# Two-block transformer kernel on one core: x also loaded already turned, and a new order for three attention units

## The reference

```python
xn = rms_norm(x, ln_mix_g)                 # x * rsqrt(mean(x*x) + eps) * g
proj = xn @ w_in                           # 1024 x 2560: u, v, q, k, v of attention
a_out = gmlp_spatial_gating(proj[..., :512], proj[..., 512:1024], ...)
b_out = banded_chunk_attention(q, k, v, q_g, k_g, rel_bias)   # 8 heads of 64
x = x + concatenate([a_out, b_out]) @ w_out
x = x + peer_ffn(rms_norm(x, ln_ffn_g), ...)   # each token: 8 heads x 16 rows of a table
# of 16384 x (1024 + 1024) floats, picked by top-k, gathered, dotted, summed
# then a second block: pooling, stick-breaking attention, memory attention, three gates, feed-forward
```

## Time and profile before

| | |
|---|---|
| median of 3 runs | 1152.63 us (1152.09 to 1153.28) |
| the profiled execution | 1152.65 us, of which the span of the engines' work is 1150.8 us |
| PE busy | 1052.1 us (91%), 4100 products |
| DVE busy | 770.2 us (67%) |
| ACT busy | 567.1 us (49%) |
| POOL busy | 288.6 us (25%) |
| gathered by POOL's queue | 268.45 MB, 56.3% of the engines' span |
| loaded by SP's queue | 102.65 MB, 24.1% |

### The profile page before, as it was taken

The page is one execution under the profiler, slowest core; times in us unless marked ns, Lnnn a source line. Parts: engine busy times, 40 slices in busy tenths (PEclk is TensorE's granted clock), DMA queues, the critical chain, the costliest instruction groups (busy, mean ns, idle before and its releaser), DMA issues.

```text
span 1150.8 us, 11796 instructions
## 1 busy us (share of the span) xinstructions
PE 1052.1 (91%) x4100; PEld 669.8 (58%) x4100; DVE 770.2 (67%) x1501; ACT 567.1 (49%) x1235; POOL 288.6 (25%) x261
## 2 busy tenths in 40 slices
PE   8999999998898779799887877889999999999998
PEld 7888554454354234344332322359878778888886
DVE  5788767667666657676676665564675596777743
ACT  7664644444543443643444345354765455444432
POOL 0001445444534424454443444400000000000000
PEclk9999999999999999999999999999999999999999
DMA  9848999999999999999999999977443454555540
GB/s 353 332 164 346 389 421 421 422 421 422 421 421 422 421 421 421 422 420 422 421 422 421 422 421 420 420 305 268 181 147 140 153 192 157 185 185 196 195 154 36
DMA packets 55531, 371.85 MB, mean 323 GB/s; under 512 B 6192, under 2 KB 7344, under 8 KB 12080
## 3 DMA queue, kind: packets, MB, share of 16 engines
q0 software_dynamic: 36864, 268.45, 56.3%
q1 hardware_dynamic: 18608, 102.65, 24.1%
HBM read 370.03 MB, written 1.05 MB: 322 GB/s over the span
## 4 chain that ended last, share of the span: by engine, by line
PE 55%; DMA 30%; DVE 6%; ACT 5%; issue 2%; POOL 1%; DVEq 0%; POOLq 0%; ACTq 0%
DMA uv<-in_peer_uv,eidx 30%; PE bank L2298 13%; PE bank L1980 8%; PE bank L1982 8%; PE bank L1981 8%; PE bank L2474 6%; PE bank L2052 4%; PE bank L2473 3%; DVE uv L1589 3%; DVE w_lo L1300 1%; PE bank L1951 1%; ACT diag L1038 1%; POOL uv L742 1%; ACT chosen L1035 1%; PE bank L2175 1%
## 5 line engine op out<-in xcount | busy, mean ns | idle before, releaser
L2298 PE MATMUL bank<-uv,diag 128*128 128x512 f32 x1024 | 490.1, 613 | 85.2 <-ACT diag L1038 84.8
L1589 DVE SCALAR_TENSOR_TENSOR uv<-uv,xn 128x1024 f32<-128x1024 f32 x256 | 313.7, 1226 | 210.4 <-DMA uv<-in_peer_uv,eidx 210.3
L742 POOL DMA_INDIRECT uv<-in_peer_uv,eidx x256 | 288.3, 1126 | 457.4 <-PE bank L2298 333.2
L2298 PEld LDWEIGHTS bank<-uv,diag 128*128 128x128 f32 x1024 | 183.6, 192 | 354.5 <-ACT diag L1038 200.5
L1300 DVE TENSOR_TENSOR w_lo<-wraw,w_hi 128x2048 fp32r<-128x2048 f32 x69 | 157.6, 2289 | 92.8 <-ACT w_hi L818 92.8
L1030 ACT ACTIVATE chosen<-chosen 128x1 f32<-128x1 f32 x256 | 51.8, 202 | 330.5 <-DVE uv L1589 330.1
L818 ACT CAST w_hi<-wraw 128x2048 fp32r<-128x2048 f32 x69 | 131.6, 1908 | 123.7 <-PE bank L2474 62.0
L2474 PE MATMUL bank<-nT_both,w_hi 128*128 128x512 f32 x320 | 109.6, 396 | 0.0
L1038 ACT ACTIVATE diag<-const,chosen 128x128 f32<-128x128 f32 x256 | 102.8, 401 | 8.3
L1035 ACT ACTIVATE chosen<-chosen 128x1 f32<-128x1 f32 x256 | 75.3, 294 | 9.3
L2473 PE MATMUL bank<-nT_both,w_lo 128*128 128x256 f32 x280 | 78.1, 279 | 0.0
(11 more groups left out here) (332 smaller groups left out, 1372.2 us busy)
## 6 DMA issues: line engine op xcount, KB each, us to landing
wraw<-in_ff_in SPq DMA_DIRECT2D x22, 1024.0 KB, 4.7
wraw<-in_ff_out SPq DMA_DIRECT2D x11, 1024.0 KB, 4.8
wraw<-in_query SPq DMA_DIRECT2D x4, 1024.0 KB, 5.3
uv<-in_peer_uv,eidx POOLq DMA_INDIRECT x256, 15.0
wraw<-in_in_q SPq DMA_DIRECT2D x2, 1024.0 KB, 7.4
wraw<-in_in_k SPq DMA_DIRECT2D x2, 1024.0 KB, 8.8
wraw<-in_pool_o SPq DMA_DIRECT2D x2, 1024.0 KB, 4.8
wraw<-in_sb_o SPq DMA_DIRECT2D x2, 1024.0 KB, 4.8
```

The source lines that it names most:

```text
L742: pool.indirect_dma_start(out=uv[:, ROW_SLOT[n], :], out_offset=None, in_=io["peer_uv"], in_offset=bass.IndirectOffsetOnAxis(ap=eidx[:, he ...
L1589: nc.vector.scalar_tensor_tensor(out=u, in0=u, scalar=1.0, in1=xn[:, head // PEER_HEADS, :], op0=ALU.mult, op1=ALU.mult, accum_out=hdot[he ...
L2298: mm = nc.tensor.matmul(acc[m][:, :], diag[:, n % RING, :], uv[:, ROW_SLOT[n], D + m * HALF:D + (m + 1) * HALF], start=False, stop=(n == R ...
```

## The change

x is brought a second time, turned on the host (`io["xT"]`), in four pieces of 256 KB, into the tile that held the gained values before (`xg`). TensorE's 16 transposes, the four banks that they took and DVE's `gained_T` go. ACT rounds x chunk by chunk (128x128) with the channel's gain as its scale, DVE takes the rest chunk by chunk, also with the gain, and the first triples wait for one chunk each. Chunks and quarters of weights alternate on both engines. `keep_warm` does 11 products where it did 6. in2a and in2b are loaded and split in quarters too. x as it is, needed for the squares, comes after in2b; ACT splits in3a before it reads the first products. The loads of the constants and of some small tensors move back. In the attention, units 0 and 1 are divided before the maxima of unit 2 are taken.

```diff
@@ -63,7 +63,7 @@
-PIECED = ("in1a", "in1b", "in2_vb")
+PIECED = ("in1a", "in1b", "in2a", "in2b", "in2_vb")
@@ -145,7 +145,8 @@
-    uses, count, turn, held = {}, [0] * 8, {}, set()
+    uses, count, held = {}, [0] * 8, set()
+    turn = {tuple(range(8)): NT * 2}
@@ -163,7 +164,6 @@
-    both("xT")
@@ -279,8 +279,7 @@
-    keys = [("xT", t, h) for h in range(2) for t in range(NT)]
-    keys += [("oT", 0), ("aT", 0), ("aT", 1), ("oT", 1)]
+    keys = [("oT", 0), ("aT", 0), ("aT", 1), ("oT", 1)]
@@ -491,6 +490,8 @@
         half_normed = sem("half_normed")
+        xT_loaded = [[sem(f"xT_loaded{t}{h}") for h in range(2)] for t in range(NT)]
+        x_rounded = [sem(f"x_rounded{t}") for t in range(NT)]
@@ -655,22 +656,29 @@
+            def load_xT(t, h):
+                sp.dma_start(xg[:, t, 4 * h:4 * h + 4, :], io["xT"][:, t, 4 * h:4 * h + 4, :]).then_inc(xT_loaded[t][h], 16)
             sp.dma_start(const[:, 0:C0], io["const"][:, 0:C0]).then_inc(ident_loaded, 16)
-            load_x(0)
-            for q in range(2):
+            load_xT(0, 0)
+            for q in range(KC // 2):
                 load_piece("in1a", q)
-            load_x(1)
-            for q in range(2, KC // 2):
-                load_piece("in1a", q)
-            for q in range(KC // 2):
+            load_xT(1, 0)
+            load_piece("in1b", 0)
+            load_xT(0, 1)
+            for q in range(1, KC // 2):
                 load_piece("in1b", q)
-            load_blocks("in2a", "in2b")
-            sp.dma_start(const[:, C0:C0 + 3 * P + 768], io["const"][:, C0:C0 + 3 * P + 768]).then_inc(const_loaded, 16)
+            load_xT(1, 1)
+            for name in ("in2a", "in2b"):
+                for q in range(KC // 2):
+                    load_piece(name, q)
+            for t in range(NT):
+                load_x(t)
+            load_block("in3a")
+            load_block("in3b")
             sp.dma_start(gmlp_g[:, :], bass.AP(tensor=g.tensor, offset=g.offset, ap=[[0, P], [1, HALF]])).then_inc(a_loaded, 16)
-            load_block("in3a")
-            load_block("in3b")
@@ -679,7 +687,9 @@
             sp.dma_start(sub_kT[:, :, :], io["sub_kT"]).then_inc(subk_loaded, 16)
-            load_blocks("out0a", "query1")
+            load_blocks("out0a", "out0b")
+            sp.dma_start(const[:, C0:C0 + 3 * P + 768], io["const"][:, C0:C0 + 3 * P + 768]).then_inc(const_loaded, 16)
+            load_blocks("out1a", "query1")
@@ -822,6 +832,8 @@
                 raw = wait_piece(act, name, q)
+                if q == 0 and name == "in2b":
+                    act.wait_ge(w_part, PART_AT[SLOT_OF[name]])
@@ -852,32 +864,39 @@
             load_table(ACT.Sqrt)
-            def round_x(t, h):
-                assert rounded["xT", t, h] == turned[0]
-                turned[0] += 1
-                wait_read(act, "xT", t, h)
-                nc.scalar.copy(aT_hi[t][:, 4 * h:4 * h + 4, :], xg[:, t, 4 * h:4 * h + 4, :]).then_inc(act_rounded, 1)
-            split_piece("in1a", 0)
-            round_x(0, 0)
+            def round_x(t, c):
+                if c % 4 == 0:
+                    act.wait_ge(xT_loaded[t][c // 4], 16)
+                nc.scalar.activation(aT_hi[t][:, c, :], xg[:, t, c, :], ACT.Copy,
+                                     scale=mix_col[:, c:c + 1]).then_inc(x_rounded[t], 1)
+            act.wait_ge(ident_loaded, 16)
+            for q in range(KC // 2):
+                round_x(0, q)
+                split_piece("in1a", q)
+            for c in range(KC // 2):
+                round_x(1, c)
+            split_piece("in1b", 0)
+            for c in range(KC // 2, KC):
+                round_x(0, c)
             for q in range(1, KC // 2):
-                split_piece("in1a", q)
-            for t, h in ((1, 0), (0, 1), (1, 1)):
-                round_x(t, h)
-            for q in range(KC // 2):
                 split_piece("in1b", q)
-            split_to("in2a")
+            for c in range(KC // 2, KC):
+                round_x(1, c)
+            for name in ("in2a", "in2b"):
+                for q in range(KC // 2):
+                    split_piece(name, q)
                 root(0, t)
+            split_to("in3a")
-            split_to("in2b")
@@ -886,7 +905,6 @@
             load_table(ACT.Sqrt)
-            split_to("in3a")
@@ -1330,34 +1348,29 @@
-            def gained_T(t, h):
-                src = wait_full(dve, "xT", t, h)
-                nc.vector.tensor_tensor(xg[:, t, 4 * h:4 * h + 4, :], four(src[:, :]), columns(mix_col, h),
-                                        ALU.mult).then_inc(read_of("xT", t, h), 1)
-            def rest_x(t, h):
-                dve.wait_ge(act_rounded, rounded["xT", t, h] + 1)
-                where = (slice(None), slice(4 * h, 4 * h + 4), slice(None))
-                nc.vector.tensor_tensor(aT_lo[t][where], xg[:, t, 4 * h:4 * h + 4, :], aT_hi[t][where].bitcast(F32),
-                                        ALU.subtract).then_inc(x_turned[t], 1)
+            def rest_x(t, c):
+                dve.wait_ge(x_rounded[t], c + 1)
+                nc.vector.scalar_tensor_tensor(out=aT_lo[t][:, c, :], in0=xg[:, t, c, :], scalar=mix_col[:, c:c + 1],
+                                               in1=aT_hi[t][:, c, :].bitcast(F32), op0=ALU.mult,
+                                               op1=ALU.subtract).then_inc(x_turned[t], 1)
             dve.wait_ge(ident_loaded, 16)
-            gained_T(0, 0)
-            split_piece("in1a", 0)
-            rest_x(0, 0)
+            for q in range(KC // 2):
+                rest_x(0, q)
+                split_piece("in1a", q)
+            for c in range(KC // 2):
+                rest_x(1, c)
+            split_piece("in1b", 0)
+            for c in range(KC // 2, KC):
+                rest_x(0, c)
             for q in range(1, KC // 2):
-                split_piece("in1a", q)
-            gained_T(1, 0)
-            gained_T(0, 1)
-            rest_x(1, 0)
-            gained_T(1, 1)
-            rest_x(0, 1)
-            rest_x(1, 1)
-            for q in range(KC // 2):
                 split_piece("in1b", q)
-            split_to("in2a")
+            for c in range(KC // 2, KC):
+                rest_x(1, c)
+            for name in ("in2a", "in2b"):
+                for q in range(KC // 2):
+                    split_piece(name, q)
@@ -1453,10 +1466,12 @@
-            for u in range(3):
+            for u in range(2):
                 maxima(u)
-            for u in range(3):
+            for u in range(2):
                 normalise(u)
+            maxima(2)
+            normalise(2)
@@ -1951,11 +1966,10 @@
-            def keep_warm(turns, *key):
-                dst = open_bank(*key)
+            def keep_warm(turns):
                 for _ in range(turns):
-                    nc.tensor.matmul(dst[:, 0:P], ident, ident, start=True, stop=True)
+                    nc.tensor.matmul(bank[0][:, 0:P], ident, ident, start=True, stop=True)
@@ -1998,13 +2012,16 @@
                     if turned == "xT":
-                        pe.wait_ge(x_turned[t], part + 1)
+                        if part or t:
+                            pe.wait_ge(x_turned[t], (part + 1) * (KC // 2))
                             between()
+                        if name == "in1a" and t == 0:
+                            pe.wait_ge(x_turned[t], c + 1)
@@ -2065,19 +2082,10 @@
             pe.wait_ge(ident_loaded, 16)
-            keep_warm(6, "xT", 0, 0)
-            def turn_x(t):
-                pe.wait_ge(x_loaded[t], 16)
-                for h in range(2):
-                    transposes(x_sb[:, t, half(h)], "xT", t, h)
-            turn_x(0)
+            keep_warm(11)
                 for p in "ab":
-                    tokens_out(f"in{n}{p}", mixing, lambda t, n=n: ("proj", n, t), turned="xT" if n == 1 else None,
-                               between=(lambda: turn_x(1)) if (n, p) == (1, "a") else None, between_at=1)
+                    tokens_out(f"in{n}{p}", mixing, lambda t, n=n: ("proj", n, t), turned="xT" if n == 1 else None)
@@ -2553,6 +2561,7 @@
     io["x"] = a["x"][0]
+    io["xT"] = a["x"][0].reshape(NT, P, KC, P).transpose(3, 0, 2, 1)
```

## The result

The median is 1156.22 us (15 runs, 1154.01 to 1158.85) against 1153.4 us of the kernel before on the same chip (15 runs, 1151.86 to 1155.17). The ratio is 1.0026, with a 95% interval of 1.002 to 1.0033. The kernel became slower by some 3 us; the forecast was 1150.0 us, within 1148.0 to 1153.0. The profiled execution of after took 1158.85 us with a span of 1157.0, and is the slowest of its runs, so single rows of it are somewhat worse than the typical execution.

A forecast was written before the change was run, and what follows sets the result against it. TensorE up to about 114 us was taken as the bound, ahead of gathers of fixed length. A start gain of 3.3 us less 0.7 us for the units made -2.6 us: 1150.0 us, range 1148.0 to 1153.0.

The forecast's parts named there:

- What bounds the kernel: TensorE before about 114 us, then gathers of fixed length; a microsecond won or lost before then comes out whole.
- Burst and clock: Start: 11 warming products take 5.37 us, to 8.1 us; the clock rises at about the burst's end, gain 3.3 us.
- The first rival: At the start the clock rises as late as before: gain 1.5 us, less 0.7, so 1151.8 us; chance 0.2.
- The eight triples of in1a: Behind the burst they follow without a break, 0.71 us each, 5.7 us in all, ending at 13.8 us for 17.12.
- Do the operands come in time?: Feed of the start: pieces land and are split before TensorE asks; the added small instructions cost nothing.
- a margin of 1.2: DVE ends in3b at 34.5 us, TensorE wants it at 35.7: 1.2 us, the narrowest margin of the stage.
- the fourth rival: The start is starved: TensorE stalls on weights at 35 us; 2.9 us slower than before, 1155.5 us; chance 0.1.
- a wait on w_lo: Sign of a starved start: a PE wait near 35 us would show that the forecast is wrong.
- ACT catches up: Behind in3b, ACT was to make up its lateness, since it waits for TensorE anyhow.
- Net loss: 0.85 - 0.17 = 0.7 us: Attention units' new order: TensorE stands 0.85 us for unit 0's copy; a 0.17 us wait at unit 1's turning goes.
- The upper end of 2.2 us: Bound on the units' loss, if the whole lateness of ACT's copies reaches TensorE.
- The sum.: Whole kernel: start -3.3 us and units +0.7 make -2.6 us, from 1152.65 to a forecast of 1150.0 us.

The follow-up runs named there:

- best_start_burst6: The changed kernel with old order of units, in4b loaded earlier, in3b copied right after in3a, pieces stored as 256 KB stretches, and 6 warming products for 11: 1149.46 us.
- contiguous3: The changed kernel with the old order of units, in4b loaded earlier and early pieces stored as stretches of 256 KB: 1150.25 us, ratio 0.9972 to the kernel before.
- best_start: The changed kernel with old order of units, in4b loaded earlier, in3b copied right after in3a, pieces stored as 256 KB stretches: 1149.46 us, ratio 0.9968.
- units_back: The changed kernel with the old order of the three attention units, all else kept: 1152.4 us, ratio 0.9997 to the kernel before.
- gelu_first3: The changed kernel with ACT's table, gelu_u(0) and copies of units 0 and 1 ahead of unit 2's exponentials: 1154.42 us, ratio 1.0014.
- units_alone: The kernel before with only the new order of the three units: 1155.89 us, ratio 1.0022.
- in2_whole: The changed kernel with in2a and in2b loaded and split whole in place of quarters: 1155.81 us, ratio 1.0023.
- units_filled3: The kernel before with the new order of units and ten unused identity products on TensorE before scores(3): 1154.39 us, ratio 1.0014.

## Why the prediction was wrong, step by step

**What bounds the kernel: right.** A microsecond of TensorE before the w_out products comes out whole, to within about 1.5 us (the table above).

**Burst and clock: right in the number, the reason not shown.** The burst's row has 5.07 us for the 5.37 forecast. The clock rose in the first triple, from 0.49 us between products to 0.23 at 7.97 us, that is at the burst's end, as chosen. The first rival falls. But the prediction chose that because the gap before the first triple goes, and best_start_burst6 speaks against the reason: its burst ends at 5.62 us, TensorE then stands 0.83 us, and behind the first product the distance is 0.24 us from 6.76 us on. Neither the longer burst nor a closed gap was needed. What held the kernel before at the slow level until 12.4 us is open, and that the chosen moment came out is in part luck.

**The eight triples of in1a: too short.** From 7.48 to 14.86 us they took 7.4 us for the 5.7 forecast. The landings of in1a's quarters were too early in the forecast: ACT waited three times for them (2.2 us in total). The gain at in1b is 2.1 for 3.3 us. With contiguous rows in1b begins at 13.39 (contiguous3) and 13.04 us (best_start), 3.6 and 3.9 us earlier than before, and in best_start TensorE keeps them up to q and k (51.12 for 55.04). So the 3.3 us were there, and the rate was the mis-sized term.

**"Do the operands come in time?": failed.** The step took 400 GB/s from in2b's landing for all that is loaded, the small pieces too. They came at 278. ACT's 128x128 operations, the other doubt of that step, cost what was assumed (1.28 / 4 = 0.32 us back to back; DVE's rest 1.14 / 4 = 0.28), and TensorE waited 0.2 us for them in all. In3b was split at 38.6 us for the forecast 34.5, and a margin of 1.2 became a loss of 1.85 (1.97 - 0.23, and 0.11 for the slower restart). In units_back and gelu_first3, the same up to there, in3b was split at 37.1 us and TensorE waited 0.4 and 1.3 us: 2.6 us later than forecast is the typical size, 4.1 that of this one execution. This is the fourth rival's mechanism at a smaller size, with its sign, a wait on w_lo, at 37 us. The forecast stopped looking behind in3b ("ACT catches up"); in4b, 5.2 us later here and 3.0 in units_back (40.4 for 37.4 us), kept DVE late to the units, worth 0.9 us.

**"Net loss: 0.85 - 0.17 = 0.7 us": failed.** It cost 3.1 us for 0.7. The lateness of ACT was right: counted from unit 0's exponentials, its copies come 2.2 us later (70.14 - 63.59 before, 72.92 - 64.14 in units_alone). But the first that waited wasn't the copy. Scores(3), one step earlier on TensorE, write into the bank from which gelu_u(0) reads, bank 0, that of proj(0, 0). The kernel before has room there, and so no wait in its trace. From its timelines of ACT and PE, gelu_u(0) and scores(3):

```profile
69.57 0.67 ACT L926 ACTIVATE u_sb<-bank,stat 128x512 f32<-128x512 f32 x1
```
```profile
71.02 1.14 PE L2096 MATMUL bank<-kT,qT 64*128 64x256 f32 x8
```

The read ends at 70.24, 0.8 us ahead, so I did not see that dependence; the bank order in the code shows it. The sum could have been done from these rows: 2.2 us later is 72.4, scores(3) are due at 70.85 (0.17 earlier, as forecast), a stall of 1.6, which is what units_alone shows. The clock's fall behind it was in no term, 1.5 us. The upper end of 2.2 us was a bound on the lateness of one engine, and the stall plus the clock go past it.

**The sum.** Start: forecast -3.3, measured -0.4, within noise of nothing. Units: forecast +0.7, measured +3.1 on the kernel before and +3.2 on the new start. The start is the larger error, 2.9 us for 2.5, and the two make up the 2.8 us measured (-0.4 + 3.2). Each error alone would have stayed in the range: 1152.65 - 3.3 + 3.1 is 1152.5, and 1152.65 - 0.4 + 0.7 is 1153.0. They came together, and the chances had counted them one at a time.

## What to carry to other kernels

Here each engine takes its steps in a fixed order: whoever puts a step later asks first what stands behind it on the next engine, and which banks these read, since a dependence that is met leaves no wait in the trace. A stall of TensorE can cost more than its length: behind three of the stalls in these runs, though not behind others as long, the products ran at the slow level. When a start is rebuilt from more and smaller transfers, take the rate of transfers with the same row length and pitch, not that of whole blocks.

## What the runs showed of the hardware

**The clock after a short stall.** Stalls of 1.6 us (units_alone) and 2.35 us (after, and in2_whole) were followed by products at half rate. In after the granted clock is 0.66 over the 5 us behind it, in units_alone 0.80 and 0.86 in the stretches from 70 and 75 us, in units_filled3 1.00. In stretches of 1 us it is 0.50 from 77 to 79 us in after and from 73 to 76 in units_alone: the fall from 2.4 to 1.2 GHz. In gelu_first3 stalls of 1.3 and 1.8 us showed no fall (1.00), nor did after's own of 1.6 us at 37 us (0.23 us between products behind it), so not every one of this length brings it; which do isn't settled. The Trainium skill, TensorE: Matmul & The Clock Gate, section "What's actually happening", has these two levels, and the trace agrees: 0.23 us from product to product of 512 columns at the one, 0.43 at the other (the kernel before, at 9.37 and 9.80 us).

**Rows of 2 KB, 8 KB apart.** Of the new start, the six profiles with such pieces have 278 to 300 GB/s in 5 to 11 us, and the four with contiguous ones 355 to 392; the engines' share is 0.93 to 1.01 in the six and 1.03 to 1.05 in the four. The old start, with fewer such pieces in that stretch, has 307 to 340, and 367 with contiguous ones. The Trainium skill, DMA: Bandwidth & Descriptors, section "Bandwidth", asks for 1 MiB or more in a transfer; here pieces of 256 KB moved at up to 392 GB/s once contiguous, and in2_whole's larger loads won nothing, so the trace does not bear the rule out at this size. From 20 us on, whole blocks move at 396 to 408 in after, before and best_start alike. Why the pitch matters in the early pieces is open, and of in4b's 5.2 us delay in after only some 3.5 are accounted for (1.1 for 448 KB more ahead of it, 2.4 for 0.95 MB less moved by 40 us).

**A transfer's issue can take long.** The issue of in4a on SP took 8.24 us in after, where most take 0.43. It took 3.9 to 8.2 us in all ten profiles of the new start and 1.4 to 2.2 in the four of the old one. In after in4b is issued right behind it and two others, 1.75 us later than before (28.77 for 27.02), so it is part of in4b's delay. No experiment changed it, and best_start is fast with an issue of 7.2 us, so what it costs is open:

```profile
19.33 8.24 SPq L638 DMA_DIRECT2D wraw<-in_in4a x1
```
